# A hybrid decoder layer: input projections by seven products instead of eight, in three passes, with GpSimd making the sums of h

## The reference, cut to what matters

```python
h = rms_norm(x, pre_g)
z = h @ w_in                      # 24 tiles of 128 columns
u = cc * ch
y_conv = cb * short_conv(u) * jax.nn.silu(cz)
y_swa = swa_attention(q, k, v, ...) * jax.nn.silu(sz)   # window 128, ALiBi, sinks
mk, mv = (rms_norm(mem, mem_g) @ w_mk, rms_norm(mem, mem_g) @ w_mv)
y_mem = mem_attention(mq, mk, mv) * jax.nn.silu(mz)
y = jnp.concatenate([y_conv, y_swa, y_mem], axis=-1) @ w_out
return x + rms_norm(y, post_g)
```

## Time and profile before

| what | us |
|---|---|
| median of 3 runs (854.34 to 855.33) | 855.19 |
| span of the profiled execution | 853.6 |
| TensorE busy in it | 845.1 |
| GpSimd, VectorE, ScalarE busy | 600.4, 467.1, 242.9 |

### The profile page before, as it was taken

One profiled execution on the slowest core, in us unless ns is written; L12 is line 12 of the kernel. 1 busy time (PEld: TensorE's weight loads), 2 busy tenths in 40 slices (PEclk: granted clock), 3 DMA queues, 4 the chain that ended last, 5 costly groups with the idle time before them and its releaser, 6 DMA issues.

```text
span 853.6 us, 13888 instructions
## 1 busy us (share of the span) xinstructions
PE 845.1 (99%) x5306; PEld 706.8 (83%) x5306; DVE 467.1 (55%) x1020; ACT 242.9 (28%) x669; POOL 600.4 (70%) x802
## 2 busy tenths in 40 slices
PE   9999999999999999999999999999999999999997
PEld 8999999998877877887887778777777887787785
DVE  6428777976352556676543436765445054577414
ACT  6523413312110444232211323431121134224111
POOL 5799575666888666766969675767388985766771
PEclk9999999999999999999999999999999999999999
DMA  9764322127356233216566422222643732222232
GB/s 336 271 223 157 125 74 75 51 63 296 124 173 247 99 99 124 69 56 184 199 194 226 148 99 99 75 74 38 222 130 103 249 106 74 76 74 75 67 155 99
DMA packets 39906, 115.87 MB, mean 136 GB/s; under 512 B 6624, under 2 KB 13024, under 8 KB 39424
## 3 DMA queue, kind: packets, MB, share of 16 engines
q1 hardware_dynamic: 39552, 114.71, 40.2%
q10 hardware_dynamic: 288, 0.27, 0.1%
HBM read 105.73 MB, written 10.26 MB: 136 GB/s over the span
## 4 chain that ended last, share of the span: by engine, by line
PE 92%; POOL 3%; DMA 2%; SPq 1%; DVE 0%; issue 0%; ACT 0%; DVEq 0%; POOLq 0%; ACTq 0%
PE pj L667 68%; PE pa L667 21%; POOL w_lo L619 2%; DMA w_raw<-in_weights 2%; PE pa L819 2%; PE pa L775 1%; POOL w_hi L616 1%; SPq L504 0%; PE pa L693 0%; DVE w_lo L1276 0%; SPq L505 0%; SPq L502 0%; SPq L506 0%; SPq L451 0%; SPq L503 0%
## 5 line engine op out<-in xcount | busy, mean ns | idle before, releaser
L619 POOL TENSOR_TENSOR w_lo<-w_raw,w_hi 128x256 fp32r<-128x256 f32 x516 | 413.5, 832 | 10.8
L667 PE MATMUL pj<-h_hi,w_hi 128*128 128x512 f32 (+2 forms) x936 | 334.1, 357 | 1.8 <-POOL w_lo L619 1.0
L667 PE MATMUL pj<-h_hi,w_lo 128*128 128x512 f32 (+2 forms) x936 | 328.4, 351 | 0.0
L667 PE MATMUL pj<-h_lo,w_hi 128*128 128x512 f32 (+2 forms) x936 | 328.1, 351 | 0.0
L616 POOL TENSOR_SCALAR w_hi<-w_raw 128x512 fp32r<-128x512 f32 x258 | 170.4, 679 | 195.3 <-PE pj L667 155.3
L667 PEld LDWEIGHTS pj<-h_hi,w_hi 128*128 128x128 f32 x936 | 176.4, 188 | 32.2 <-issue 10.1
L667 PEld LDWEIGHTS pj<-h_hi,w_lo 128*128 128x128 f32 x936 | 176.3, 188 | 23.2
L667 PEld LDWEIGHTS pj<-h_lo,w_hi 128*128 128x128 f32 x936 | 176.5, 189 | 21.4
L667 PE MATMUL pa<-w_hi,y_hi 128*128 128x512 f32 x160 | 62.6, 392 | 0.0
L667 PE MATMUL pa<-w_lo,y_hi 128*128 128x512 f32 x160 | 62.4, 390 | 0.0
L667 PE MATMUL pa<-w_hi,y_lo 128*128 128x512 f32 x160 | 62.2, 389 | 0.0
(11 more groups left out here) (212 smaller groups left out, 1012.0 us busy)
## 6 DMA issues: line engine op xcount, KB each, us to landing
w_raw<-in_weights SPq DMA_DIRECT2D x131, 512.0 KB, 3.6
res<-in_x_prompt SPq DMA_DIRECT2D x16, 512.0 KB, 7.5
out_y_prompt<-o_nat SPq DMA_DIRECT2D x15, 512.0 KB, 5.8
x_row<-in_x_prompt SPq DMA_DIRECT2D x12, 512.0 KB, 3.7
x_t<-in_xt SPq DMA_DIRECT2D x12, 512.0 KB, 6.0
first_rows<-in_x_prompt SPq DMA_DIRECT2D x4, 512.0 KB, 10.7
mkt_s<-in_mkt SPq DMA_DIRECT2D x2, 1024.0 KB, 5.0
memv_c<-in_cache_mv SPq DMA_DIRECT2D x4, 512.0 KB, 7.3
```

The costliest lines, as they stand in the source:

```text
L619: last = pool.tensor_tensor(w_lo[slot][:, part], raw[:, part], w_hi[slot][:, part].bitcast(F32), ALU.subtract)
L667: return pe.matmul(out, lhsT, rhs, start=start, stop=stop)
```

## The change

The program is written anew around the input projection; nearly all names of the attention, the samples and the convolution stay.

*Seven products.* Two of the 24 tiles form a pair (`PAIRS`), the width is cut in halves of 512 (4 k-tiles) and the rows of a pass in halves: a 2 x 2 by 2 x 2 product of blocks. It is made of seven block products and sums before and after them (Winograd's form of Strassen's scheme). A product is 4 k-tiles x 3 terms of 348 (last pass 344) columns. The sums of the weights (`w_sum`, four a pair) are made by VectorE in pass 0 and stored to DRAM for the other passes; the sums of results are spread over ScalarE (copies of banks), VectorE (c11, c12, c21) and GpSimd (c22).

*Three passes* of 664, 696 and 688 prompt rows, the sample rows in the first. Products are numbered: 84 a pass (12 pairs x 7, the first two pairs interleaved), 8 products of the memory in pass 0, 260 in all; then 128 parts of the output projection, last, after all passes. The words "slot n" mean what each engine does for product n. All results go to DRAM (`proj_d`), and attention reads them back, a pass behind, one visit each 12 or 13 slots from slot 104.

*Splitting.* A weight tile is 128 x 512. ScalarE now makes w_hi and GpSimd w_lo, in a ring of five, five products ahead. The seven right-hand operands (h_hi, h_lo for products 1 to 7) stand whole in SBUF and are written over at the change of pass, each after its last product.

*Sums of h.* Operands 5, 6, 7 and 4 are differences of quarters of h. For pass 0 VectorE makes them; for passes 1 and 2 GpSimd does (`t_sum`), four subtractions of 348 each, before or while the last pair's products run.

*Row factors.* All now go over DRAM: `write_rstds`, then `load_r1` (pass 0, both chunks), rsm (memory) and rs (passes 1 and 2). In pass 0 results are scaled after the product (`times_r`, c21, `c22_r`).

```diff
-            def split(n):
-                slot, raw = n % WS, w_raw[n % RAW]
-                pool.wait_ge(w_loaded[n % RAW], (n // RAW + 1) * 16)
-                if n >= WS:
-
-                    pool.wait_ge(proj_done, last_unit(SEQ[n - WS]))
-                for part in halves:
-                    done = step(pool.tensor_scalar(w_hi[slot][:, part], raw[:, part], 1.0, 1.0, ALU.mult, ALU.mult))
-                need(done)
-                for part in quarters:
-                    last = pool.tensor_tensor(w_lo[slot][:, part], raw[:, part], w_hi[slot][:, part].bitcast(F32),
-                                              ALU.subtract)
-                last.then_inc(w_split, 1)
+            def split(n):
+
+                for i, part in enumerate(halves):
+                    if i == 0 or n == 0:
+                        pool.wait_ge(w_his, n + 2 if n else 1 + i)
+                    if i == 0 and n >= WS:
+                        pool.wait_ge(prod_done, n - WS + 1)
+                    pool.tensor_tensor(w_lo[n % WS][:, part], raw_of(n)[:, part], w_hi[n % WS][:, part].bitcast(F32),
+                                       ALU.subtract).then_inc(w_split, 1)
+            def t_sum(p, m):
+
+                w = NW[p]
+                if m == 5:
+                    pool.wait_ge(scaled_x, 16 * (p - 1) + 8)
+                    pool.wait_ge(h_ready[4], 3 + p)
+                elif m == 7:
+                    pool.wait_ge(scaled_x, 16 * p)
+                elif m == 6:
+                    pool.wait_ge(h_ready[1], 4 + p)
+                else:
+                    pool.wait_ge(h_ready[5], 4 + p)
...
+                for k in range(4):
+                    cols = slice(k * w, (k + 1) * w)
+                    last = pool.tensor_tensor(out[:, cols], x[:, cols], other[:, cols], ALU.subtract)
+                last.then_inc(staged, 1)
+            for n in range(NEND + 4):
+                if n + 5 < NPROD:
+                    split(n + 5)
...
+                for g in range(NG):
+                    if n == SL[g, 7]:
+                        token = c22(g)
...
+                if n in T_AT:
+                    t_sum(*T_AT[n])
+    for _m, _n in ((5, SL[_last, 1] - 4), (7, SL[_last, 1] - 2), (6, SL[_last, 1] + 1), (4, SL[_last, 5] + 1)):
+        T_AT[_n] = (_p, _m)
```

The products, and ScalarE's part of them:

```diff
+            def product(n):
+                g, m = PROD[n]
...
+                if opens:
+                    wait_chain(pe, BEFORE[g, c])
+                else:
+                    pe.wait_ge(copied, COPIED[g, {6: 1, 7: 6, 4: 7, 3: 5}[m]])
+                new = FIRST_USE[p, m] == n
+                if new and p:
+                    pe.wait_ge(h_ready[m], 4 + p)
+            def hi_refill(p, m):
+                w = NW[p]
+                act.wait_ge(prod_done, SL[NPAIR * p - 1, m] + 1)
+                if m in SCALED:
+                    act.wait_ge(scaled_x, 16 * (p - 1) + SCALED[m])
+                else:
+                    act.wait_ge(staged, 4 * (p - 1) + STAGED[m])
+                copy(h_hi[m][:, 0:4 * w], staged_in[m][:, 0:4 * w]).then_inc(h_his, 1)
+            for n in range(9, NEND):
+                if n < NPROD and isinstance(PROD[n][0], int):
+                    copy_of(n)
+                if n + 5 < NPROD:
+                    hi(n + 5)
...
+                if n in REFILL_HI:
+                    hi_refill(*REFILL_HI[n])
...
+                if n == 14:
+                    act.wait_ge(r1_loaded, 2 * 16)
+                    act.activation(r2[:], r1[:], ACT.Square).then_inc(r2_made, 1)
```

The row factors of pass 0, on SP's queue:

```diff
+            def write_rstds(group):
+                a, b = SPAN[group]
+                sp.wait_ge(rstds, GROUP[group])
+                if group == "a":
+                    sp.dma_start(rs_d[0, 0:6 * P].rearrange("(b p) -> p b", p=P), rstd[:, a:a + 6],
+                                 allow_slow_non_contiguous=True).then_inc(rs_written, 16)
...
+            def load_r1():
+                sp.wait_ge(rs_written, 2 * 16)
+                sp.dma_start(r1[:, 0:PT[0]], rs_d[:, 0:PT[0]].to_broadcast([P, PT[0]])).then_inc(r1_loaded, 16)
+                sp.dma_start(r1[:, PT[0]:], rs_d[:, SEQ_LEN:SEQ_LEN + NS].to_broadcast([P, NS])).then_inc(r1_loaded, 16)
...
+                if n == 11:
+                    write_rstds("a")
+                if n == 12:
+                    load_r1()
```

2737 lines of the change are left out of this document (1518 added, 1219 removed).

## The result

The changed kernel takes 1015.83 us (median of 4 runs, 1013.14 to 1019.11) against 854.91 us: 1.188 times the time before, 95% interval 1.185 to 1.192. The forecast was 869 us with a range of 840 to 892.

The account below looks back on a forecast made before the run. TensorE's matmul list was taken as the bound: 853.6 us less 60.3 saved, with small corrections, gave 792.8 uninterrupted; interruptions counted as 75 made 867.8, and 1.6 more gave 869 us, range 840 to 892.

Parts of the forecast that it names:

- Product pace: Sign in the input products: matmuls of 348 columns 158 to 159 ns apart where nothing holds them, a product 1.90 us.
- The places of the holds: Signs of where TensorE would wait: h near 10 to 45 us, r1 near 60 us, w_lo and a copy at pass changes.
- The first 14 products: Start of pass 0: ScalarE's queue makes the 14th product end at 47.8 us, not 33.5: +14 us (10 to 20).
- The row scales go by way of DRAM: Pass 0: single-word writes delay r1 and product 18, +15 us (11 to 18); the memory rows repeat this, +4 (0 to 10).
- the rest: Gated pairs, three buffers for all stores to DRAM, and 16 output tiles split within 9 slots: +5 us (0 to 12).
- The sums of h: GpSimd's sums at the changes to passes 1 and 2 hold TensorE: +18 us (12 to 26) and +16 (10 to 22).
- In passes 1 and 2 GpSimd needs 10.9 + 1.5 us of 13.3 a group: hidden: Passes 1 and 2: GpSimd's work fits within each group of products, so no time was added for it.
- +3 for pass 0: GpSimd in pass 0: subtractions for w_lo and sums of results, slowed beside VectorE, were to cost +3 us (0 to 8).
- The lead covers the sums: Rival: holds overlap and engines run ahead, pass changes cost only GpSimd's own sums less lead: 840 us, faster; chance 24%.
- Held engines, slower clock: Rival: a slower clock with held engines, its middle 892 us; chance 14%.
- The weight load: Rival: the 348-column matmul is bound by its weight load, an instruction of 188 ns: +90 us, 959 us; chance 1%.

Follow-up runs that it names:

- e7: Eight sums of weights of pairs 0 and 1 moved from VectorE to GpSimd, against the changed kernel (1015.83 us): 1023.68 us.
- e3: Row scales written to DRAM in pieces of 8 to 40 bytes, not single words (result differs from the reference), against the changed kernel: 999.42 us.
- e6: Row scales of pass 0 and memory spread by TensorE transposes without DRAM, those of passes 1 and 2 written in 512-byte pieces, against the changed kernel: 984.79 us.
- e5: Six buffers in place of three for finished quarters in pass 0, against the changed kernel: 997.49 us.
- e9: Four edits on the changed kernel: sums of h on VectorE, six buffers in pass 0, row scales spread by TensorE, output stores at slot 236: 957.92 us.
- e2: GpSimd makes only 8 of 348 columns of each sum in passes 1 and 2 (sums unfinished), against the changed kernel: 993.40 us.
- e1: Sums of h in passes 1 and 2 moved from GpSimd to VectorE at the same slots, against the changed kernel: 1001.65 us.
- e10: Half of GpSimd's w_lo subtractions left out from product 98 on (low parts half stale), against the changed kernel: 981.60 us.
- e8: TensorE executes additional 348-column products before its waits for products 7, 18, 23, 25 and 54, against the changed kernel: 1019.56 us.

## Why the prediction was wrong

*What held.* Product pace: matmuls of 348 columns are 0.158 to 0.16 us apart where nothing holds them, 1.90 us a product. The output projection came out 2 us off. The places of the holds were named right: near 10 to 45 us for h, before product 18 for r1 with ScalarE idle (it waited 15.0 us), at the first change of pass for w_lo (7.25 us) and for ScalarE's copy (4.62 us, and not 5 or more), with ScalarE waiting 14.9 us for a GpSimd sum. The sign was right.

*"The first 14 products", +14: mis-sized.* Product 14 started at 58.4 and not 47.8. The sum counted ScalarE's queue, 34.9 us of work and 6.4 of waits; the chain that ended last alternates between ScalarE and VectorE instead (x scaled, subtracted, rounded, the rest taken, a weight sum between), and VectorE is busy 43 of 58 us. The chain between 26 and 42 us (start, us, what):

```profile
27.32 1.52 ACT quad L1280 x3
...
35.13 1.46 DVE h_lo L1564 x2
...
38.35 2.92 DVE temp L1583 x4
...
41.70 0.45 ACT copies L1280
```

No experiment shortened it: that moving the weight sums away makes it worse is shown (e7), that the alternation is the cause is read from the chain only.

*"The row scales go by way of DRAM", +15 and +4: the mechanism right, its reach wrong.* r came at 76.5 us and not at 67, because its write was issued at 59.2 and not at 48.1, behind the late start above; the write (11.8 us) and the spread (5.5) took what the forecast gave them (12 and 6). But the mistake that counts is that each write of single words was costed as a delay to its own reader. Three stores to proj lie right behind the second write and one behind the third; they hold the three buffers, the buffers hold VectorE, and VectorE ScalarE's copies: holds of 9.9 and 13.6 us. A third, of 7.0, ends with a store too, behind 1 MB of weight sums and the end of 2 MB of memory weights; larger pieces did not shorten it (7.4 in e3), none at all did (4.7 in e6). And the hold of 13.6 us is 8.0 in e6, so part of it belongs to the large transfers in front of that store. The forecast had all this under "the rest" as part of +5, from transfers of 3.6 to 7.5 us that no small pieces went ahead of. The rows to see it were there: such writes keep the queue 9.4 us each. e6 took 31 us back, e5 18, and e9 with both 42 up to product 85 and, with the sums moved, 51 up to product 98.

*"The sums of h", +18 and +16: about right.* The first change of pass took 24.5 us over its products (13 of 1.90), the second some 14 (nine); a good quarter of it stays when the sums are left out, so the sums themselves were priced too high. All sums together cost the kernel 22 us (e2), 14 of them because it is GpSimd that makes them (e1). The +18 also had each of VectorE's seven h_lo hold GpSimd, a term that no run shows: beside the one of 12.69 us GpSimd kept 0.70 us a rounding, two others ran while it had nothing to do (322.9 to 330.9 us), beside two, with other work of VectorE's between them, its four subtractions took 7.36 us in place of 3.58, and beside the last two its roundings took 1.19 us each. The largest terms of the forecast were the least of its problems.

*"In passes 1 and 2 GpSimd needs 10.9 + 1.5 us of 13.3 a group: hidden": the step that failed most.* That is 93% of an engine: 14 roundings at the 0.708 us of one alone, a sum of 0.96, and 1.5 us of waits for VectorE. Measured in this stretch were 0.856 us a rounding on average, 0.98 where a visit's softmax runs, and 1.03 for the sum of results: 13.0 us of 13.3 a group. So the slack that was to hide it, 0.9 us a group, is nearly gone. And an average over a group hides the stretches of 5 to 10 us in which GpSimd has roundings queued without a gap: there VectorE's two-input instructions take twice their time (0.83 to 0.88 us in place of 0.40 to 0.42), and TensorE waits for their results, 3.9 us in all for GpSimd's own. Of the 66 us missing, and of the 84 over products and visits, e10 shows 41 to follow from GpSimd's roundings. The others are open: in e10 TensorE still waits 9.4 us for probabilities, 8.5 for copies, 8.2 for the memory's sum and 4.1 for ev, and no run took one of these away alone. The forecast read the same slowing off and charged it to GpSimd alone, a price for each VectorE instruction by its columns that is in its +3 for pass 0, in its +18 and in the 1.5 us here. No row and no run shows such a price. The trace before has three VectorE instructions of 512 columns at 1.11, 1.10 and 1.22 us from 202.56 us on, beside GpSimd, and three at 0.69, 0.75 and 0.69 just before; four that read PSUM (211.23 to 215.31 us) take 0.69 us each beside it. What the trace after shows is 0.906 us a rounding from 58.4 to 288 us (126 of them, 25 us over the 0.708 of one alone), and the 0.856 here. VectorE's side of it, a longer softmax in front of TensorE's turn (671 ns a prob, 508 in e10), was left out.

*The rivals.* "The lead covers the sums" is refuted by every hold above; its 15.4 is 16 subtractions of 348 columns at 0.96 us, which took 18.6 us at the first change, and its 6.2 a lead of 4 x 1.90 - 1.42. "Held engines, slower clock" was right that the clock is lower after a hold: the product behind a hold takes 3.65 us at a granted clock of 0.50, one that nothing held 1.91 at 1.00, and the mean clock is 0.917, before 0.999. No run shows the 23 us that make its 892 of the forecast's 869; the slow matmuls add up to 36 us. How much of that is hidden behind other waits is not shown; the two products that e8 did make faster gained nothing. The weight load is no bound: where nothing holds them, matmuls start 0.158 us apart, below the 0.20 us of a load (0.19 in the earlier trace rows).

## What to carry to other kernels

A change that makes the matmul list shorter leaves every other engine's work per product unchanged, so its share of each product rises: here 1.75 us of GpSimd roundings, at what they took in this trace, against a product of 1.90. Check each supporting engine not only at its mean but where its work stands most densely, and charge both engines for the time they work side by side: here a VectorE instruction took 0.83 to 0.88 us in place of 0.40 to 0.42, a GpSimd rounding beside it 0.98 in place of 0.70. And follow a slow DMA to everything queued behind it: 256 single words put some 7 us on stores that had nothing to do with them (10.6 to 11.5 in place of a median of 4.0), while seven small transposes and two copies did the same job in 2 us.

## What the runs showed of the hardware

A VectorE instruction with two inputs in SBUF lasted 12.67 to 12.70 us in ten kernels, where the same instruction lasts 1.59 to 2.14 us elsewhere in this change of pass. Beside it GpSimd executed fifteen instructions without a gap and kept its 0.70 us a rounding; by the times of both, VectorE's stood for some 11.1 of the 12.69 us. In other places VectorE's takes twice its time (0.83 to 0.88 us in place of 0.40 to 0.42 at 256 columns), 0.43 us more where a GpSimd rounding alone lasts 0.70, and GpSimd's rounding takes 0.98. The VectorE instruction that reads PSUM (pt) kept its time, 679 ns beside all of GpSimd's roundings and 681 beside half of them (e10). What decides between the standing and the doubling was not tried.

The same was seen with a two-column copy, 8.80 us in e6 (0.17 at its shortest), and with a 344-column product, 13.68 us in e7 (0.50 at its shortest), both with GpSimd at work; neither was looked into.

Writes of single words came with late landings for the stores behind them: with 256 such words just ahead, stores of 158 to 174 KB landed after 10.6 to 11.5 us, with pieces of 8 bytes ahead (e3) after 5.5 to 6.3, with none (e6) after 1.8 to 4.0. Pieces of 8 to 40 bytes gained 16 us here, the way without DRAM 31.

The granted clock is low behind TensorE's idle times in these traces: the product behind the hold of 12.2 us took 3.64 us at a clock of 0.50, one that nothing held 1.91 us at 1.00. Filling five holds raised the mean from 0.917 to 0.943 and gained nothing, with the product behind at full clock in two of the five.
